# Prompt attention of a decoder layer: four value products for a unit in place of six, put behind the transposes of the same unit

## The reference

```
s  = einsum(q, k) * HEAD_DIM ** -0.5          # per block: 128 queries x 256 keys
s  = where(mask, s, -inf)
m  = maximum(max(s), sink)
e  = exp(s - m)
pr = e / (sum(e) + exp(sink - m))
o  = einsum(pr, v)                            # 128 queries x 64 for each head
yb = o * silu(za)
out: m = sigmoid(ga) * (ya @ w_proj_pool) + sigmoid(gb) * (yb @ w_proj_attn)
```

## Time and profile before

| | us |
|---|---|
| median of 3 runs (1248.48 to 1253.87) | 1252.45 |
| the profiled execution, its own time | 1255.48 |
| its span, first to last instruction | 1253.7 |
| TensorE busy | 1214.8 (97%) |
| VectorE, ScalarE, GpSimd busy | 527.6, 413.6, 410.6 |
| the 128 value products with pt_hi, the 64 with pt_lo | 45.3, 25.2 |

### The profile page before, as it was taken

The page is one execution under the profiler, slowest core; times in us unless marked ns, Lnnn a source line. Parts: engine busy times, 40 slices in busy tenths (PEclk is TensorE's granted clock), DMA queues, the critical chain, the costliest instruction groups (busy, mean ns, idle before and its releaser), DMA issues.

```text
span 1253.7 us, 19497 instructions
## 1 busy us (share of the span) xinstructions
PE 1214.8 (97%) x7676; PEld 1193.0 (95%) x7676; DVE 527.6 (42%) x881; ACT 413.6 (33%) x882; POOL 410.6 (33%) x189
## 2 busy tenths in 40 slices
PE   4899999899999999999999999999999999999997
PEld 4799889899999999999999999999999999999997
DVE  5869677200044444444433516481042251064321
ACT  3233333323267777777740101130020020041112
POOL 2323223223312222221144533424325435254410
PEclk8899989999999999999999999999999999999999
DMA  7413525532243434433351111116232233232211
GB/s 276 127 46 115 179 104 139 160 102 51 72 127 120 127 111 133 118 92 113 110 189 48 55 58 44 36 33 247 85 93 94 86 103 125 81 102 61 76 36 52
DMA packets 135948, 129.36 MB, mean 103 GB/s; under 512 B 40319, under 2 KB 123543, under 8 KB 135887
## 3 DMA queue, kind: packets, MB, share of 16 engines
q1 hardware_dynamic: 118487, 101.79, 26.9%
q10 hardware_dynamic: 17400, 26.71, 5.8%
HBM read 92.79 MB, written 37.71 MB: 104 GB/s over the span
## 4 chain that ended last, share of the span: by engine, by line
PE 88%; DVE 9%; DMA 1%; issue 1%; ACT 0%; SPq 0%; ACTq 0%; DVEq 0%
PE ps L576 75%; PE ps L765 4%; PE ps L743 2%; PE ps L753 2%; DVE sa L988 1%; DVE xn L933 1%; DVE sa L974 1%; DVE m_lo L937 1%; DVE sa L984 1%; PE ps L631 1%; DVE stack L968 1%; DVE hs L976 1%; DVE stack L966 1%; DVE sa L980 1%; PE ps L704 1%
## 5 line engine op out<-in xcount | busy, mean ns | idle before, releaser
L576 PE MATMUL ps<-m_hi,w_hi 128*128 128x352 f32 x2016 | 663.8, 330 | 8.1 <-DVE m_lo L937 8.1
L576 PE MATMUL ps<-m_lo,w_hi 128*128 128x352 f32 x2016 | 651.4, 324 | 0.0
L576 PE MATMUL ps<-m_hi,w_lo 128*128 128x352 f32 x2016 | 436.7, 325 | 0.0
L576 PEld LDWEIGHTS ps<-m_hi,w_hi 128*128 128x128 f32 x2016 | 381.9, 189 | 11.0 <-issue 5.7
L576 PEld LDWEIGHTS ps<-m_lo,w_hi 128*128 128x128 f32 x2016 | 381.8, 189 | 0.1
L576 PEld LDWEIGHTS ps<-m_hi,w_lo 128*128 128x128 f32 x2016 | 346.7, 189 | 0.0
L511 POOL TENSOR_TENSOR w_hi<-raw_a,w_one 128x1024 fp32r<-128x1024 f32 x42 | 81.2, 1934 | 778.3 <-PE ps L576 525.2
L513 POOL TENSOR_TENSOR w_lo<-raw_b,w_hi 128x1024 fp32r<-128x1024 f32 x42 | 111.0, 2643 | 3.3
L513 POOL TENSOR_TENSOR w_lo<-raw_a,w_hi 128x1024 fp32r<-128x1024 f32 x42 | 109.6, 2609 | 3.3
L511 POOL TENSOR_TENSOR w_hi<-raw_b,w_one 128x1024 fp32r<-128x1024 f32 x42 | 89.9, 2141 | 0.0
L1052 DVE TENSOR_TENSOR pt_lo<-ps,pt_hi 128x512 fp32r<-128x512 f32 x64 | 41.2, 686 | 58.5 <-ACT pt_hi L1386 58.5
(11 more groups left out here) (181 smaller groups left out, 1134.8 us busy)
## 6 DMA issues: line engine op xcount, KB each, us to landing
raw_a<-in_w_in SPq DMA_DIRECT2D x26, 512.0 KB, 3.8
raw_b<-in_w_in SPq DMA_DIRECT2D x26, 512.0 KB, 4.4
qk_d<-qkst ACTq DMA_DIRECT2D x10, 1056.0 KB, 4.1
gate_d<-gst ACTq DMA_DIRECT2D x16, 528.0 KB, 4.4
gin<-gate_d SPq DMA_DIRECT2D x16, 528.0 KB, 3.7
qt<-qk_d SPq DMA_DIRECT2D x32, 256.0 KB, 3.1
xT_d<-sa SPq DMA_DIRECT2D x4, 1056.0 KB, 7.4
yb_d<-sa SPq DMA_DIRECT2D x1, 4224.0 KB, 12.9
```

Of the source, the lines that this page charges most:

```text
L576: last = nc.tensor.matmul(ps[:, 3 * parity + c, 0:CH], w, x[:, k, CH * c:CH * c + CH], start=(k == 0 and w is wh and x is src_hi), stop=(k ...
```

## The change

`vt` has 128 columns for a key row, v_hi and v_lo side by side as they lie in memory, loaded by one DMA. A matmul then gives the product with v_hi on partitions 0 to 63 and that with v_lo on 64 to 127; with pt_hi and pt_lo and two key blocks there are four. (The product of v_lo and pt_lo, left out before, is now in it.) VectorE copies the low half to `v_low`, adds it to the high half in PSUM, and multiplies both kinds of heads from partitions 0 to 63. The transposes move up (T0 behind S1, T1 a step later), and V(u-1) stands a step behind T1 in the half of unit u. V no longer waits for pt_lo of the second block as a whole: the wait stands between its two pairs. On VectorE gate_output(u-1) stands between split_probs(u-1) and reciprocals(u).

```diff
-            vt = sb("vt", [P, 2, NKV, 2 * P], F32R, scope=s3)
+            vt = sb("vt", [P, 2, NKV, P], F32R, scope=s3)
+            v_low = sb("v_low", [HD, G * P], scope=s3)
...
-                for c in range(2):
-                    dst = vt[:, m // 4, m % 4, :].rearrange("p (s c e) -> p s c e", s=2, c=2)[:, :, c]
-                    sp.dma_start(dst.bitcast(F32), v_d[t, :, m % 4, :].rearrange("p (s e) -> p s e", s=2))\
-                        .then_inc(v_loaded[m % 4], 16)
+                sp.dma_start(vt[:, m // 4, m % 4, :].bitcast(F32), v_d[t, :, m % 4, :]).then_inc(v_loaded[m % 4], 16)
...
                 kv = m % 4
-                bank = round_of("V", u, 0, m)
-                pe.wait_ge(v_loaded[kv], t * 32 + 32)
+                r = att_round("V", u)
+                pe.wait_ge(att_read, r - 1)
+                bank = 6 + att_bank("V", m) % 2
+                pe.wait_ge(v_loaded[kv], t * 16 + 16)
...
                 for s in range(2):
-                    for a, b in ((0, pt_hi), (0, pt_lo), (1, pt_hi)):
-                        last = nc.tensor.matmul(ps[:, bank, :], vt[:, s, kv, P * a:P * a + P], b[s][:],
-                                                start=(s == 0 and a == 0 and b is pt_hi),
-                                                stop=(s == 1 and a == 1))
+                    if s:
+                        pe.wait_ge(att_read, r)
+                    for b in (pt_hi, pt_lo):
+                        last = nc.tensor.matmul(ps[:, bank, :], vt[:, s, kv, :], b[s][:],
+                                                start=(s == 0 and b is pt_hi), stop=(s == 1 and b is pt_lo))
...
-                after = {k0: [], k0 + 1: [], k0 + 2: []}
-                if not first or m >= 2:
-                    after[k0].append(lambda: values(u - 2, (m - 2) % 8, t if m % 4 >= 2 else t - 1))
+                after = {k0: [], k0 + 1: [], k0 + 2: [], k0 + 3: []}
...
                 if not first or m >= 1:
-                    after[k0 + 2] += [lambda: turn_probs(u - 1, (m - 1) % 8, 0), lambda: turn_probs(u - 1, (m - 1) % 8, 1)]
+                    after[k0 + 1].append(lambda: turn_probs(u - 1, (m - 1) % 8, 0))
+                    after[k0 + 2].append(lambda: turn_probs(u - 1, (m - 1) % 8, 1))
+                    after[k0 + 3].append(lambda: values(u - 1, (m - 1) % 8, t if m % 4 else t - 1))
...
-            pool_group(0, {0: [lambda: values(end - 2, 6, PBLK - 1)],
-                           2: [lambda: turn_probs(end - 1, 7, 0), lambda: turn_probs(end - 1, 7, 1)],
+            pool_group(0, {2: [lambda: turn_probs(end - 1, 7, 0), lambda: turn_probs(end - 1, 7, 1)],
...
+                o = ps[:, att_bank("V", m), :]
+                v.tensor_copy(v_low[:], o[HD:P]).then_inc(low_step, 1)
+                dve.wait_ge(low_step, u * 2 + 1)
+                v.tensor_tensor(o[0:HD], o[0:HD], v_low[:], ALU.add).then_inc(low_step, 1)
+                dve.wait_ge(low_step, u * 2 + 2)
                 for q in range(2):
-                    half = slice(64 * q, 64 * q + 64)
-                    o = ps[half, att_bank("V", m), :].rearrange("p (a q n) -> p q a n", q=2, n=P)[:, q]
-                    dst = sa[half, 2 * kv:2 * kv + 2, tok]
-                    last = v.tensor_tensor(dst, o, dst, ALU.mult)
+                    dst = sa[64 * q:64 * q + 64, 2 * kv:2 * kv + 2, tok]
+                    heads = o[0:HD].rearrange("p (a q n) -> p q a n", q=2, n=P)[:, q]
+                    last = v.tensor_tensor(dst, heads, dst, ALU.mult)
                 last.then_inc(att_read, 1)
...
-                if not first or m >= 2:
-
-                    tok = bass.ds(i * (2 * P) + ((m - 2) // 4) * P, P)
-                    gate_output(u - 2, (m - 2) % 8, tok)
                 mask_scores(u, m, 1 if m >= 4 else (0 if first else 2), first and m == 0)
                 if not first or m >= 1:
                     split_probs(u - 1, (m - 1) % 8)
+                    gate_output(u - 1, (m - 1) % 8, bass.ds(i * (2 * P) + ((m - 1) // 4) * P, P))
                 reciprocals(u, m)
```

More of the change, by code:

```diff
@@ L295, in build @@
             sem("key_copied"), sem("s_read"), sem("s_exp"), sem("s_recip"), sem("s_prob"), sem("spt_copied"))
-        att_done, att_read = sem("att_done"), sem("att_read")
+        att_done, att_read, low_step = sem("att_done"), sem("att_read"), sem("low_step")
         masks_loaded, zero_done = sem("masks_loaded"), sem("zero_done")
@@ L729, in round_of @@
                 if not isinstance(r, int) or r >= 2:
-                    pe.wait_ge(att_read, r if kind == "V" else r - 1)
+                    pe.wait_ge(att_read, r - 1)
                 return 6 + (att_bank(kind, m, first) + s) % 2
@@ L1087, in _ @@
             end, last_tok = PBLK * NKV, slice(SEQ - P, SEQ)
-            gate_output(end - 2, 6, last_tok)
             split_probs(end - 1, 7)
```

## The result

| | before | after |
|---|---|---|
| median, us | 1251.33 (1248.48 to 1253.87, 4 runs) | 1296.56 (1291.7 to 1297.51, 4 runs) |
| span of the profiled execution | 1253.7 | 1294.9 |
| ratio of the times, 95% interval in brackets | | 1.0359 [1.0342, 1.0375] |

A forecast was written before the change was run, and what follows sets the result against it. TensorE, full throughout attention, was taken as the bound, with VectorE's in-order path adding waits. Product saving -14.9 plus waits 57.0 gave +42 us: 1297.5 on the profiled execution, 1294.5 on the median, 1296 taken; range 1277 to 1316.

The forecast's parts named there:

- 14.9 us of products would be saved: TensorE in attention: four value products per unit in place of six, 64 fewer at 0.233 us, -14.9 us.
- Each new VectorE instruction 0.69 us: VectorE's copy and addition per unit: 0.69 us each, bounds 0.42 and 1.22.
- Normalise ends 4.60 us after TensorE goes on: ScalarE's normalise, queued behind output and reciprocals, ends 4.60 us after TensorE resumes behind the previous unit's value products.
- Transposes 0.80 late in each half: TensorE reaches a unit's transposes after 3.85 us but starts them at 4.65, waiting for normalise: 0.80 us per half.
- The gate 4.38 us, V of odd units 1.99 + 0.13 late: Odd units: ScalarE's gate delays the pt_hi copies by 4.38 us; value products wait 1.99 us, their second pair 0.13.
- B: Zero point for times within a half: the moment TensorE goes on after the previous unit's value products.
- 57 us of waits: TensorE's added waits in attention: 12.0 us in even units, 44.0 in odd, 0.97 in unit 31; together 57.0.
- Even halves 9.27, odd ones 11.40: Time from one unit's value products to the next's: 9.27 us in even units, 11.40 in odd; pair 20.67, before 18.0.
- The first rival, the clock: TensorE's clock falls to 0.50 after the recurring waits at odd units' value products: time about 1317 us, chance 0.2.
- Shorter waits: Attention waits shorter, as new VectorE instructions run faster (0.42 us each) or the gate overlaps: 1277.5 us, chance 0.12.
- Cancel: Attention waits of 9 to 21 us offset the saving, time within 0.5% of before; chance 0.03.
- faster: The path through the reciprocals is hidden and no attention wait is left: 1237.6 us, chance 0.05.

The follow-up runs named there:

- kernel with the late DMA: Changed kernel with reciprocals ahead of the output, both transposes together behind the third step, gate's DMA issued behind the next pt_hi copies: 1239.65 us, ratio 0.9909.
- doubled copy: Changed kernel with the copy to v_low made twice per unit, one behind the other: 1315.11 us, ratio 1.053.

## Why the prediction was right

- *TensorE was the bound, so 14.9 us of products would be saved.* Held. The kernel with the late DMA shows it free of waits: V to V 17.2 us a pair (483.69 to 500.88 in its timeline) against 18.0, 0.81 x 15.5 = 12.6, and 11.3 us in the time, where 0.93 a pair was expected. The missing 0.1 a pair is a start after a wait too short to show, at V in the odd unit (0.34 us from its first product, at 483.69, to the next, where 0.23 is the pace); what separates 12.6 from 11.3 is within the interval of the ratio. So of the 14.9 us about three quarters came out.
- *Each new VectorE instruction 0.69 us.* Measured 0.693 and 0.692; 64 partitions cost what 128 do at 512 columns. The bounds of 0.42 and 1.22 were far too wide.
- *Normalise ends 4.60 us after TensorE goes on.* TensorE went on at 500.86 (0.93 after 499.93), normalise ended at 505.43: 4.57.
- *Transposes 0.80 late in each half.* The profile has 0.72 of idle in this pair, and counts idle only from the end of the last matmul, 0.16 after its successor would have started: 0.88. The sum had the transposes start 0.05 us after normalise ended; they started 0.14 after it (505.43 to 505.57).
- *The gate 4.38 us, V of odd units 1.99 + 0.13 late.* Gate 4.38 again (505.43 to 509.81). V: 1.69 + 0.16 = 1.85 in the pair shown, 1.75 on average over the 15 odd units of the loop, less than worked out: V started when foretold (B+10.39 for 10.33) but was due 0.2 later, as T0 and T1 with the steps behind them had taken longer. Unit 31 waited 0.24 + 0.16 where 0.97 had been put.
- *57 us of waits.* The profile gives 44.2 of idle, with 0.16 for each of 46 waits 51.6. What the waits fell short was made up by what the sum had left out: the first product behind a wait takes 0.34 instead of 0.23 (511.25 to 511.59), in most odd units that of the second pair as well, and transposes in two places break into two steps instead of one (1.53 us for 1.45). -14.9+51.6 leaves 8.5 us for these to reach the 45.2 measured. Read from the timeline they are 0.25 us in the pair shown and about 0.34 in the next, 4 to 5 us over the stage; the rest of the 8.5 is not accounted for.
- *Even halves 9.27, odd ones 11.40.* From the end of a V to the end of the next they took 9.46 and 11.47 (512.33 to 521.79, 500.86 to 512.33). The pair was put at 20.67 and took 20.93.
- *1296.* That it came to 0.6 us of the measured time is luck. The sum gave +42 where +45.2 was measured, waits too long and restarts left out nearly cancelled, and 1296 was chosen between 1294.5 and 1297.5. What the runs bear out is the mechanism and the size to some 3 us.
- The first rival, the clock, did not come: 1.00 through attention, with sixteen waits of up to 1.7 us. The chance of 0.2 rested on one wait of 2.01 us that was followed by a fall; these are shorter. The Trainium skill, "TensorE: Matmul & The Clock Gate", "HAM oscillation", tells of waits that come round in a loop and re-throttle the array each time; the waits of its example are of about 3 to 5 us. These of up to 1.7 us did not do it. The doubled copy comes nearer to it, below.
- "Shorter waits" failed on its price: the new instructions took 0.69 us on 64 partitions, not 0.42, and the gate still began only when normalise had ended (505.45). "Cancel" and "faster" needed a path 1.5 to 2.4 us shorter, and it was 0.03 shorter: VectorE does work in order, and the reciprocals stood behind the wait. "Faster" is right in its turned form: with the reciprocals ahead, the time is within 0.25% of the kernel before, and with both transposes together and the gate's DMA later too it is 0.9% faster.

## What to carry to other kernels

On a kernel whose main engine is full, a helper engine at 42% is not spare: what counts is the longest path through it from one product of the main engine to the next, and an instruction that waits must stand behind everything that others need sooner. Here the place of one group of four instructions was worth 42 us, and their work of 71 us on VectorE (32 x 1.39 + 64 x 0.42) next to nothing once it stood off the path. Work moved earlier on the full engine has to be followed through every in-order queue that it passes, with what is queued behind it (here an unrelated gate with two table loads); once that was put right, three quarters of the saving in products came out (11.3 of 14.9 us).

## What the runs showed of the hardware that was not expected

The granted clock fell twice during attention in the kernel with the doubled copy, whose waits at V were as long as in the changed kernel and those at the transposes 0.6 us longer. Both times TensorE had just gone on from a V that had waited. The value product and the stretches of 1 us behind it (us, busy, clock, DMA share, GB/s), first the one, then the other:

```profile
450.69 0.50 PE L767 MATMUL ps<-pt_hi,vt 128*128 128x512 f32 x1 [1.63 <-DVE pt_lo L1052]
...
452.00:453.00 1.00, 1.00 (x6) 0.56 0.00 0
...
455.00:456.00 1.00, 1.00 (x7) 0.73 0.00 0
456.00:457.00 1.00, 1.00 (x9) 1.00 0.00 0
...
495.44 0.50 PE L767 MATMUL ps<-pt_hi,vt 128*128 128x512 f32 x1 [1.60 <-DVE pt_lo L1052]
...
496.00:497.00 1.00, 1.00 (x5) 0.75 0.00 0
...
499.00:500.00 1.00, 1.00 (x6) 0.54 0.00 0
```

Thirteen other V's of the same trace waited 1.5 to 1.7 us and no fall followed. The two falls cost almost nothing: the time lost at the lower clock (0.50, that is 1.2 GHz) was time that TensorE would have waited at the next transposes, and V to V is 10.41 and 10.56 us over them where it is 10.35 to 10.42 without. That is the same path once more: it ran on VectorE and ScalarE, whatever TensorE's clock was.

The length of a wait alone does not decide. Ahead of attention, in code that none of these kernels changes, TensorE waits 2.77 us for `stack` and later 2.90 us for `kts`. In the eleven profiled executions a fall to 0.50 went with the first in seven, and followed the second in all but the one of the kernel before, which is the one that the prediction had to go by the earlier trace rows. What does decide is open.

A start after a wait costs TensorE about 0.1 us over the wait itself, as the 0.34 us for 0.23 to the second product and the 2.01 for 1.91 above show; small once, and by an estimate from these 3 to 5 us over a stage with 46 of them.

ScalarE's table load before the sigmoid took 1.29 us from its start to that of the sigmoid (505.45 to 506.74), and 1.29 to 1.30 in every kernel run here that has the load (the one with a copy for the sigmoid has none). The Trainium skill, "ScalarE: Activation LUTs", "What ACT_TABLE_LOAD costs", adds a drain of about the same length to each; no row here shows it. The 31 us that the prediction estimated from it did not come: the gate took 4.38 us as before. (Put on top of that, two such drains would make it 7.1 us, by an estimate from the page's figure; the prediction's 6.4 left out the issue of the DMA and the warm-up.)
